# Feed-forwards 1 to 3 with the down projection between the gate and up units, in three fp32r passes, and modulation rows summed four to a tile

## The chip, the cores and the metric

The kernel runs on one NeuronCore of a Trainium2 chip (trn2). Its time is device microseconds of one launch, the median of several runs. A core has TensorE (matmuls into the 8 banks of PSUM), VectorE, ScalarE, GpSimd and SyncE; each works through its own list of instructions in order, and they wait for each other by semaphores. Loads are DMAs: a queue of SyncE, ScalarE or GpSimd issues one, and 16 DMA engines carry it.

## The reference, cut to what matters

Two transformer blocks in a row, each of two layers, over 256 tokens of width 1024, and 256 context tokens that only the first layer reads. All data is float32. Four SwiGLU feed-forwards belong to the first block:

```
def swiglu(h, w13, w2):                       # w13: 1024 x 5632, w2: 2816 x 1024
    a, b = jnp.split(h @ w13, 2, axis=-1)
    return (jax.nn.silu(a) * b) @ w2
def half_ffn(x, g, shift, scale, gate, w13, w2):
    return x + 0.5 * gate * swiglu(modulate(x, g, shift, scale), w13, w2)
m = (silu_c @ w_mod[i] + b_mod[i]).reshape(b, 1, N_MOD, d)     # shifts, scales and gates of a layer
```

Before the first layer's mixer a feed-forward runs over latent and context tokens (512 columns, "FFN 0"); FFN 1, 2 and 3 run over the 256 latent tokens. The modulation rows m are products of one vector with matrices of 1024 x 1024: 9 rows of each first-block layer, and 6 of each second-block layer. After them come mixers and, in the second block, two mixtures of experts (MoE) with 16 experts each.

## The kernel before

Activations lie with features on the partitions: X is 8 tiles of 128 features by up to 512 tokens. The order of the stages is fixed: first modulation rows, FFN 0, mixer a, FFN 1, FFN 2, mixer c, FFN 3, mixer e, MoE 0, mixer o, MoE 1. Between two stages stands a norm: VectorE updates X tile by tile, ScalarE squares, TensorE sums the squares (`mean_square`) and spreads the root, and VectorE and ScalarE write the normed h in two rounded parts (h high and h low).

Weights come through `ring`, four slots of 1 MB units (up to 1.4 MB). SyncE issues the load of a unit as soon as the unit four places ahead of it is done. A gate/up unit holds 128 gate and 128 up columns for all 8 feature tiles. It is split: ScalarE copies it, rounded to fp32r, into one of two buffers (L1437), and VectorE subtracts that from the unit in place (L1844), which gives the low part. TensorE then takes three fp32r products a tile, high x high, high x low and low x high (`up`, L777): 48 products of 128x128 with 256 columns a unit. There are 22 such units a feed-forward. ScalarE applies silu and VectorE multiplies gate and up parts into G.

After the 22 units come 8 down units of 1.4 MB, one for each output tile of 128 features. They are not split: one f32 product for each of 22 tiles of G (`down`, L850), which the page counts as two instructions each. FFN 0 already has its down part in three fp32r passes with split tiles (`down0`, L812); it stays as it is.

Besides, the modulation rows that are needed later are computed beside the feed-forwards. A row is a product of a vector of 1024 numbers with a 1024 x 1024 matrix, in 8 chunks of 128 matrix rows by 1024 columns (512 KB). SyncE loads a chunk into one of four buffers in CB (`chunk_in`, L577), after it has seen that the chunk four places before is added; VectorE adds chunk times a number for each partition to an accumulator of 128 x 1024 (`add_chunk`, L1878; for the three "dual" rows, which the context needs with a second vector, twice, L1868). When a row's 8 chunks are in, TensorE sums over the partitions by 8 f32 products with one column of ones (`column_sums`, L699, for dual rows 16, L709), and VectorE adds the bias (`take_row`). `CHUNKS_AT` says by hand how many chunks follow each unit; `PLAN` is made from it. There are 3 dual and 25 single rows, 224 chunks: 112 in FFN 0, 40 in FFN 1, 40 in FFN 2 and 32 in FFN 3. In SyncE's list the chunks of a unit stand behind the load of the unit two places later, in VectorE's behind the gate product of the unit and ahead of the split of a later one.

Of the kernel before, what the change touches and what calls it, by code (L numbers as in the profile page):

```python
# [7 lines left out]
ALU = mybir.AluOpType  # L8
# [6 lines left out]
P = 128  # L15
D = 1024
# [22 lines left out]
for _e in range(1, NE):  # L39
# [20 lines left out]
N_ROWS_C = 13  # L60
# [3 lines left out]
DOWN0 = _GROUPS + _GROUPS[4:] + _GROUPS[:4]  # L64
DOWN0_BANK = (0, 1, 5, 6, 2, 3, 4, 0)


N_DUAL_CHUNKS = N_DUAL * KT
# [7 lines left out]
ROW_ACC = (0, 1, 0, 1, 0, 1, 2, 0, 2, 0, 2, 0, 1, 0, 2, 3, 0, 1, 0, 2, 3, 0, 1, 2, 3)  # L76
ROW_BANK = tuple((4, 7)[r % 2] if r < 6 else 7 if r < 11 else (4, 6)[r % 2] for r in range(N_ROWS))


def chunk_plan():  # L80

    plan, n = [], 0
    for ups_at, downs_at in CHUNKS_AT:
        counts = list(ups_at) + list(downs_at)
        steps = [dict(chunks=[], sums=[], dual=[], takes=[]) for _ in counts]
        for i, count in enumerate(counts):
            for _ in range(count):
                steps[i]["chunks"].append(n)
                if n % KT == KT - 1:
                    r, at = n // KT - N_DUAL, min(i + 1, len(counts) - 2)  # L90
                    if r < 0:
                        steps[at]["dual"].append(r + N_DUAL)
                    else:
                        steps[at]["sums"].append(r)
                        steps[min(at + 1, len(counts) - 1)]["takes"].append(r)
                n += 1
        plan.append(steps)
    assert n == (N_DUAL + N_ROWS) * KT
# [6 lines left out]
def steps_after(n):  # L105

    return 2 * min(n + 1, N_DUAL_CHUNKS) + max(0, n + 1 - N_DUAL_CHUNKS)

# [3 lines left out]
    ("up1", FT), ("down1", KT), ("up2", FT), ("down2", KT), ("c_in", 8), ("c_out", 4),  # L112
    ("up3", FT), ("down3", KT), ("e_in", 14), ("e_out", 4), ("moe0", NE * 6),
# [21 lines left out]
for _name, _n in (("up0", FT), ("down0", len(DOWN0)), ("up1", FT), ("up2", FT), ("c_in", 8), ("up3", FT), ("e_in", 14), ("moe0", 6 * NE), ("o_in", 12),  # L135
# [15 lines left out]
for _name, _n in _COLS:  # L151
# [6 lines left out]
         ("rot_half", P), ("upper", P), ("ones", P), ("zeros", P), ("w4", 8), ("w16", 32), ("iota", CAP),  # L158
# [26 lines left out]
MOD_RUNS = ((0, N_FIRST * KT), (N_FIRST * KT, ROW_TILE0))  # L185
# [2210 lines left out]
```

## Time and profile before

| | |
|---|---|
| median of 3 runs (2500.26 to 2511.84) | 2507.69 us |
| the profiled execution's own time | 2501.64 us |
| its span, first to last instruction | 2499.8 us |
| busy: TensorE, VectorE, ScalarE | 96%, 57%, 40% |
| mean granted clock of TensorE, share of 2.4 GHz | 0.958 |
| moved by DMA, mean rate | 535.45 MB, 214 GB/s |
| PE L777 (gate/up), L850 (down), L699 (row sums), shares of the chain | 25%, 9%, 2% |
| FFN 0, from its first product to the mixer's first | 422 us |
| FFN 1, 2 and 3, up to the next stage's first product | 223, 223, 219 us |

The profile's shares of busy time are means over all stages. "PE" is TensorE's matmul, "PEld" its weight loads, "DVE" VectorE, "ACT" ScalarE, "SPq" the queue in which SyncE issues DMAs. The chain is the run of work that ended last, followed back step by step.

### The profile page before, as it was taken

What the parts mean: (1) busy time and instruction counts of PE and PEld (TensorE: products, weight loads), DVE (VectorE), ACT (ScalarE), POOL (GpSimd) and SP (SyncE); (2) the same over time, 40 slices, a digit from 0 to 9 for tenths busy, and PEclk for the clock granted to TensorE, in tenths of its full rate; (3) what the DMA queues carried; (4) which work ended last, traced back from release to release, by engine and by line L of the source; (5) the groups of instructions that cost most, each with busy time, mean ns of one, the idle gap of its engine ahead of it and who ended that gap; (6) DMA issues with size and microseconds to landing.
All of it is one profiled execution on the core that took longest, in us unless ns stands there. A gap on an engine that the chain in (4) does not pass through costs nothing.

```text
span 2499.8 us, 35746 instructions
## 1 busy us (share of the span) xinstructions
PE 2397.4 (96%) x15358; PEld 2158.7 (86%) x15358; DVE 1430.5 (57%) x1609; ACT 1000.5 (40%) x1257; POOL 4.5 (0%) x12
## 2 busy tenths in 40 slices
PE   9999999989999999999999988899999899899997
PEld 7788888867998999888998986899998888899996
DVE  0875676323763465234652442688887433888886
ACT  2211132214330332042321323577776344676774
POOL 0000000000000000000000000000000000000000
PEclk8999999989999999999999988899999789899998
DMA  7456767522777477543775431488886332488884
GB/s 277 172 196 240 265 227 271 192 68 79 259 279 277 171 292 294 186 152 129 262 276 212 151 118 37 148 300 294 300 305 242 142 121 75 179 304 295 296 307 180
DMA packets 94195, 535.45 MB, mean 214 GB/s; under 512 B 9984, under 2 KB 12296, under 8 KB 46800
## 3 DMA queue, kind: packets, MB, share of 16 engines
q1 hardware_dynamic: 92480, 524.33, 58.3%
q0 software_dynamic: 816, 5.65, 0.6%
q8 instruction: 126, 2.06, 0.3%
q10 hardware_dynamic: 736, 3.10, 0.3%
q14 instruction: 37, 0.30, 0.0%
HBM read 531.97 MB, written 1.06 MB: 213 GB/s over the span
## 4 chain that ended last, share of the span: by engine, by line
PE 90%; DVE 6%; ACT 3%; issue 1%; DVEq 0%; ACTq 0%
PE PS L777 25%; PE PS L1231 12%; PE PS L850 9%; PE PS L888 8%; PE PS L1259 7%; PE PS L812 5%; PE PS L935 5%; DVE moe_low L2202 2%; PE PS L1199 2%; PE PS L733 2%; PE PS L699 2%; PE PS L1179 1%; PE PS L659 1%; PE PS L742 1%; PE PS L876 1%
## 5 line engine op out<-in xcount | busy, mean ns | idle before, releaser
L777 PE MATMUL PS<-h_parts,ring_low 128*128 128x256 f32 (+1 forms) x1408 | 440.0, 313 | 0.0
L777 PE MATMUL PS<-h_parts,g_parts 128*128 128x256 f32 x2112 | 383.0, 284 | 0.9 <-DVE h_parts L1813 0.9
L2202 DVE TENSOR_TENSOR moe_low<-moe_ring,W_HIGH 128x2048 fp32r<-128x2048 f32 x128 | 292.9, 2290 | 83.1 <-ACT W_HIGH L1615 83.1
L777 PEld LDWEIGHTS PS<-h_parts,g_parts 128*128 128x128 f32 x2112 | 328.9, 192 | 2.4 <-issue 1.2
L1231 PE MATMUL PS<-moe_low,HXH 128*96 128x256 f32 x1024 | 287.9, 281 | 0.0
L777 PEld LDWEIGHTS PS<-h_parts,ring_low 128*128 128x128 f32 x1408 | 269.9, 192 | 16.1
L1615 ACT ACTIVATE W_HIGH<-moe_ring 128x2048 fp32r<-128x2048 f32 x128 | 244.5, 1912 | 23.4 <-PE PS L1259 22.7
L850 PE MATMUL PS<-G,ring 128*128 128x256 f32 x1056 | 236.5, 385 | 2.8 <-DVE G L1898 2.8
L850 PEld LDWEIGHTS PS<-G,ring 128*128 128x128 f32 x1056 | 201.3, 192 | 30.7 <-DVE G L1898 3.4
L1460 ACT ACTIVATE SG<-PS 128x256 f32<-128x256 f32 (+1 forms) x88 | 38.4, 437 | 462.9 <-PE PS L777 462.9
L1231 PEld LDWEIGHTS PS<-moe_low,HXH 128*96 128x96 f32 x1024 | 166.2, 162 | 0.3
L1898 DVE TENSOR_TENSOR G<-SG,PS 128x256 f32<-128x256 f32 (+1 forms) x88 | 43.0, 488 | 208.4 <-ACT SG L1460 208.4
L1844 DVE TENSOR_TENSOR ring_low<-ring,g_parts 128x2048 fp32r<-128x2048 f32 x66 | 150.9, 2291 | 18.8 <-ACT g_parts L1437 17.9
L2202 DVE TENSOR_TENSOR moe_low<-moe_ring,h_parts 128x2048 fp32r<-128x2048 f32 x64 | 146.3, 2286 | 4.0 <-ACT h_parts L1615 1.5
L1231 PE MATMUL PS<-W_HIGH,HXL 128*96 128x256 f32 x528 | 148.0, 280 | 0.0
L1231 PE MATMUL PS<-W_HIGH,HXH 128*96 128x256 f32 x528 | 148.0, 280 | 0.0
L1878 DVE SCALAR_TENSOR_TENSOR CAT<-CB,cond_rows,CAT 128x1024 f32<-128x1024 f32 x112 | 143.5, 1281 | 5.9
L777 PE MATMUL PS<-h_parts,W_HIGH 128*128 128x512 f32 x352 | 141.9, 403 | 3.5 <-DVE H_LOW L1809 3.5
L1231 PE MATMUL PS<-h_parts,HXH 128*96 128x256 f32 x496 | 142.4, 287 | 0.0
L777 PE MATMUL PS<-H_LOW,W_HIGH 128*128 128x512 f32 x352 | 141.5, 402 | 0.0
L1231 PE MATMUL PS<-h_parts,HXL 128*96 128x256 f32 x496 | 139.1, 280 | 0.0
L1437 ACT ACTIVATE g_parts<-ring 128x2048 fp32r<-128x2048 f32 x66 | 125.6, 1905 | 2.1 <-DMA ring<-up_w 2.1
(316 smaller groups left out, 4653.6 us busy)
## 6 DMA issues: line engine op xcount, KB each, us to landing
moe_ring<-moe_w SPq DMA_DIRECT2D x192, 1024.0 KB, 4.9
CB<-mod_rows SPq DMA_DIRECT2D x200, 512.0 KB, 5.9
ring<-up_w SPq DMA_DIRECT2D x88, 1024.0 KB, 5.0
ring<-lin_w SPq DMA_DIRECT2D x55, 1024.0 KB, 4.9
ring<-down_w SPq DMA_DIRECT2D x24, 1408.0 KB, 6.0
CB<-mod_dual SPq DMA_DIRECT2D x24, 512.0 KB, 4.1
ring<-down_w SPq DMA_DIRECT2D x10, 1024.0 KB, 7.8
ring<-mod_w SPq DMA_DIRECT2D x8, 1024.0 KB, 7.0
```

The lines of the kernel that those rows point to most:

```text
L777: return mm(dst(h), a[:, k, h * P:(h + 1) * P], b[:, k, :], start=start, stop=(k == KT - 1 and j == 2), skip_group_check=True)
L812: last = mm(PS[:, DOWN0_BANK[4 * half + d], :], a[:, t, d, :], b, start=(v % 6 + t + i == 0), stop=(final and t == len(tiles) - 1 and i == 2),
L850: last = mm(PS[:, i % 4, 0:S], ring[:, u % SLOTS, j * P:(j + 1) * P], G[:, j, 0:S], start=(j == 0), stop=(j == FT - 1))
L888: last = mm(dst, a, b, start=(k + j == 0), stop=(k + j == KT + len(pairs) - 2))
L935: last = mm(PS[:, i, c * S:(c + 1) * S], w[:, k, c * P:(c + 1) * P], CAT[:, k, :], start=(k == 0), stop=(k == KT - 1))
L1231: last = mm(PS[0:CAP, 2 + f % 2, 0:S], a[:, x], w[:, k, :], start=(k + i == 0), stop=(k + i == KT + 1))
L1259: last = mm(PS[0:CAP, n, :].rearrange("p (a c) -> p a c", a=2), x[:, part_g], w[:, cut, :], start=(h + f + i == 0), stop=(h + f + i == 4), ...
L1437: af(UP_HIGH[i % 2], by_tile(ring[:, u % SLOTS, 0:UW]), ACT.Copy).then_inc(w_high, 1)
L1615: af(w_high_tiles(p), by_tile(moe_ring[:, moe_slot(l, p), :]), ACT.Copy).then_inc(w_high, 1)
L1844: tt(by_tile(ring_low[:, u % SLOTS, 0:UW]), by_tile(ring[:, u % SLOTS, 0:UW]), UP_HIGH[i % 2], ALU.subtract).then_inc(w_low, 1)
L1878: stt(out=acc, in0=w, scalar=c, in1=acc, op0=ALU.mult, op1=ALU.add).then_inc(acc_steps, 1)
L2202: tt(by_tile(moe_low[:, moe_slot(l, p), :]), by_tile(moe_ring[:, moe_slot(l, p), :]), w_high_tiles(p), ALU.subtract).then_inc(w_low, 1)
```

## The change

Feed-forwards 1 to 3 (`FFN_UNITS`): four gate/up units, then nine times a down unit and two gate/up units, then the last two down units: 33 units of 1 MB. A down unit m holds the weights of two hidden tiles, 2m and 2m+1, for all 8 output tiles; its load takes eight pieces of 1 KB for a partition. Every unit is split into rounded parts, with four buffers for the high part instead of two (`FFN_HIGH`, in G's space). The product of gate and up is kept for six tiles only (`GATED`) and split as well, by a copy on ScalarE and a subtraction on VectorE. The down products take three fp32r passes and accumulate over all 11 down units in eight half banks of PSUM (`Y_BANK`). In the last unit the output tiles are finished one after another, and VectorE updates X meanwhile. Mean squares stand behind tile 6 of it (two) and behind it (six). The first two splits of the next stage move into the last two units.

Modulation rows: groups of four rows share an accumulator. A chunk now holds, for each of the four rows, 32 rows of its matrix, one row's part in 32 partitions each; a group takes 32 chunks, seven groups make 224 chunks. TensorE's sum for a group has four columns on the right (`block`), which add up 32 partitions each, so 8 products serve four rows (16 in group 0, where all four rows are computed with both vectors). The vector's numbers come in the new order by four small loads on GpSimd's queue (`cond_raw`). `CHUNKS_AT` is new: 104 chunks in FFN 0 and 40 in each other one. Nothing changes in the mixers and in MoE.

```diff
+ROWS, PARTS = 4, 32
+GROUP_CHUNKS = KT * P // PARTS
+N_GROUPS = (N_DUAL + N_ROWS) // ROWS
...
+FFN_UNITS = [("up", i) for i in range(4)]
+for _m in range(FT // 2 - 2):
+    FFN_UNITS += [("down", _m), ("up", 2 * _m + 4), ("up", 2 * _m + 5)]
+FFN_UNITS += [("down", FT // 2 - 2), ("down", FT // 2 - 1)]
+FFN_BUFFER0 = (0, 0, 33, 1)
+Y_BANK = ((4, 0), (4, 1), (5, 0), (5, 1), (6, 0), (6, 1), (7, 0), (2, 0))
...
-    ([3] * 8 + [4] * 9 + [3] * 4 + [0], [4] * 5 + [2] + [4, 2] + [4] * 3 + [0]),
-    ([1, 1, 2] * 6 + [1, 1, 0, 0], [3, 2, 3, 2, 2, 2, 0, 0]),
-    ([1, 1, 2] * 6 + [1, 1, 0, 0], [3, 2, 3, 2, 2, 2, 0, 0]),
-    ([1] * 20 + [0, 0], [2] * 6 + [0, 0]),
+    ([3] * 10 + [2] + [4] * 8 + [0, 4, 0], [4] * 5 + [2, 4, 2, 0, 4, 4, 0]),
+    ([1] * 4 + [2, 1, 1] * 5 + [0, 1, 1] + [2, 1, 1] * 3 + [2, 0], []),
+    ([1] * 4 + [2, 1, 1] * 3 + [0, 1, 1] + [2, 1, 1] * 5 + [2, 0], []),
+    ([2] * 4 + [0, 1, 1] + [2, 1, 1] * 7 + [2] + [0] * 4, []),
...
             def chunk_in(n):
-                src = mod_dual[n] if n < N_DUAL_CHUNKS else mod_rows[n - N_DUAL_CHUNKS]
+
+                g, k, part = n // GROUP_CHUNKS, n % GROUP_CHUNKS // ROWS, slice(n % ROWS * PARTS, (n % ROWS + 1) * PARTS)
                 if n >= 4:
                     sp.wait_ge(acc_steps, steps_after(n - 4))
-                sp.dma_start(ROWS_W[:, n % 4, :], src).then_inc(rows_full[n % 4], 16)
+
+                def put(j, rows, src):
+                    dst = ROWS_W[j * PARTS:(j + rows) * PARTS, n % 4, :]
+                    sp.dma_start(dst, src).then_inc(rows_full[n % 4], 16)
+                if g == 0:
+                    put(0, N_DUAL, mod_dual[k::KT, part, :])
+                    put(N_DUAL, 1, mod_rows[k:k + 1, part, :])
+                else:
+                    r0 = ROWS * (g - 1) + 1
+                    put(0, ROWS, mod_rows[r0 * KT + k:(r0 + ROWS - 1) * KT + k + 1:KT, part, :])
 
             def ffn(f):
...
+                    kind, at = FFN_UNITS[i]
+                    if kind == "up":
+                        return UW, source(up_w, FT * f + at)
+                    part = down_w[KT * f:KT * (f + 1), :, 2 * at * P:2 * (at + 1) * P]
+                    return UW, part.rearrange("d p n -> p d n")
...
+            def column_sums(g):
+                pe.wait_ge(acc_steps, steps_after((g + 1) * GROUP_CHUNKS - 1))
+                wait(pe, rows_taken, g)
+                for j in range(1 if g else 2):
+                    acc = ACC if g else DUAL_ACC[:, j, :]
+                    for d in range(KT):
+                        at = j * ROWS * KT + d
+                        last = mm(PS[:, GROUP_BANK[g], at:at + 3 * KT + 1:KT], acc[:, d * P:(d + 1) * P],
+                                  tab("block")[:, 0:ROWS], start=True, stop=True)
                 last.then_inc(colsum_done, 1)
 
-            def dual_column_sums(r):
...
+                        high, low = down_tiles(high), down_tiles(low)
+                        def products(t, d):
+                            j = 2 * i + t
+                            pe.wait_ge(g_low, FT * f + j + 1)
+                            (bank, half), at = Y_BANK[d], j % 6
+                            pairs = ((high, GATED_HIGH), (high, GATED_LOW), (low, GATED_HIGH))
+                            for p, (a, b) in enumerate(pairs):
+                                last = mm(PS[:, bank, half * S:(half + 1) * S], a[:, t, d, :], b[:, at, :],
+                                          start=(j + p + half == 0), stop=(j == FT - 1 and p == 2),
+                                          skip_group_check=True)
+                            return last
+                        if i < FT // 2 - 1:
+                            for t in range(2):
+                                for d in range(KT):
+                                    last = products(t, d)
+                        else:
+                            for d in range(KT):
+                                for t in range(2):
+                                    last = products(t, d)
+                                if d in (1, 3, 5, 6):
+                                    last.then_inc(y0_psum, 1)
+                                if d == 6:
+                                    mean_square(AFTER_DOWN[f], 0)
+                                    mean_square(AFTER_DOWN[f], 1)
                     last.then_inc(unit_done, 1)
-                    if i:
-                        mean_square(AFTER_DOWN[f], i - 1)
...
+                    sums(f, n)
+                for d in range(2, KT - 1):
+                    mean_square(AFTER_DOWN[f], d)
...
+            def ffn(f):
+
+                def gated_high(i):
+                    act.wait_ge(g_ready, FT * f + i + 1)
+                    af(GATED_HIGH[:, i % 6, :], GATED[:, i % 6, :], ACT.Copy).then_inc(g_high, 1)
+                units = len(FFN_UNITS)
+                for n, (kind, i) in enumerate(FFN_UNITS):
+                    if n + 2 < units:
+                        split(f, n + 2)
+                    else:
+                        split_next(f, n + 2 - units)
+                    if n and FFN_UNITS[n - 1][0] == "up":
+                        gated_high(FFN_UNITS[n - 1][1])
+                    if kind == "up":
+                        act.wait_ge(unit_done, UNIT0[f"ffn{f}"] + n + 1)
+                        af(SG[:, i % 4, 0:S], PS[:, i % 2, 0:S], ACT.Silu).then_inc(silu_ready, 1)
 
...
+            for part in range(ROWS):
+                src = bass.AP(cols_in.tensor, part * PARTS * NCOLS, [[0, ROWS], [NCOLS, PARTS], [1, 4 * KT]])
+                pool.dma_start(cond_raw[:, part, :], src).then_inc(ld_cond, 16)
...
+                for j in range(1 if g else 2):
+                    acc = ACC if g else DUAL_ACC[:, j, :]
+                    at = 4 * (m // ROWS) + (group_cond(g) if g else j)
+                    c = cond_rows[:, m % ROWS, at:at + 1]
+                    if m == 0:
+                        if g > 1:
+                            dve.wait_ge(colsum_done, g)
+                        ts(acc, w, c, None, ALU.mult).then_inc(acc_steps, 1)
+                    else:
+                        dve.wait_ge(acc_steps, steps_after(n - 1) if g else 2 * n - 1 + j)
+                        stt(out=acc, in0=w, scalar=c, in1=acc, op0=ALU.mult, op1=ALU.add).then_inc(acc_steps, 1)
...
+                def gated_low(i):
+                    dve.wait_ge(g_high, FT * f + i + 1)
+                    tt(GATED_LOW[:, i % 6, :], GATED[:, i % 6, :], GATED_HIGH[:, i % 6, :], ALU.subtract).then_inc(g_low, 1)
+                units = len(FFN_UNITS)
+                for n, (kind, i) in enumerate(FFN_UNITS):
+                    if n + 2 < units:
+                        split(f, n + 2)
+                    else:
+                        split_next(f, n + 2 - units)
+                    if n and FFN_UNITS[n - 1][0] == "up":
+                        gated_low(FFN_UNITS[n - 1][1])
+                    if kind == "up":
+                        dve.wait_ge(silu_ready, FT * f + i + 1)
+                        tt(GATED[:, i % 6, :], SG[:, i % 4, 0:S], PS[:, i % 2, S:2 * S], ALU.mult).then_inc(g_ready, 1)
+                    if n == units - 2:
+                        gate_columns(f)
+                    rows_step(PLAN[f][n])
+                for d in range(KT):
+                    if d == KT - 1:
+                        dve.wait_ge(unit_done, UNIT0[f"ffn{f}"] + units)
+                    else:
+                        dve.wait_ge(y0_psum, 6 + 4 * (f - 1) + (1, 1, 2, 2, 3, 3, 4)[d])
+                    bank, half = Y_BANK[d]
+                    update(f, d, bank, half * S)
 
             def gate_columns(f):
                 N = NORMS[FFNS[f][0]][0]
```

## Rows read from the trace of the kernel before

**Rows 1.** The page, busy us of each engine.

```profile
PE 2397.4 (96%) x15358; PEld 2158.7 (86%) x15358; DVE 1430.5 (57%) x1609; ACT 1000.5 (40%) x1257; POOL 4.5 (0%) x12
```

**Rows 2.** Windows: stretch, length, busy by engine, PEclk, DMA share, GB/s.

```profile
65.60:339.70 274.10, 274.08 (x1249) 225.31 (x1250) 184.20 (x173) 57.35 (x57) 0.00 (x0) 0.97 0.63 219
...
626.90:760.60 133.70, 132.78 (x1104) 132.06 (x1103) 88.91 (x84) 47.82 (x49) 0.00 (x0) 1.00 0.75 273
...
836.00:838.00 2.00, 2.00 (x6) 1.56 (x5) 0.37 (x2) 0.00 (x0) 0.00 (x0) 0.50 0.45 174
```

**Rows 3.** The chain in order of time: start us, us, what.

```profile
112.69 3.47 PE PS L709 x32
...
154.27 24.63 PE PS L777 x96
...
375.02 22.45 PE PS L812 x96
...
399.15 22.40 PE PS L812 x96
...
487.63 7.14 PE PS L876 x32
...
626.89 40.63 PE PS L777 x336
...
705.75 34.87 PE PS L777 x288
...
742.30 17.39 PE PS L777 x144
...
760.60 19.26 PE PS L850 x88
...
780.20 9.60 PE PS L850 x44
...
833.49 11.29 PE PS L850 x44
...
849.48 41.11 PE PS L777 x336
...
1072.56 6.33 PE PS L876 x48
...
1170.80 52.41 PE PS L777 x432
...
1389.76 6.33 PE PS L876 x48
```

**Rows 4.** VectorE from 626 to 1400 us: group | busy us, mean ns.

```profile
L1844 DVE TENSOR_TENSOR ring_low<-ring,g_parts 128x2048 fp32r<-128x2048 f32 x64 | 146.4, 2291 | 16.5 <-ACT g_parts L1437 15.6
...
L1878 DVE SCALAR_TENSOR_TENSOR CAT<-CB,cond_rows,CAT 128x1024 f32<-128x1024 f32 x56 | 71.6, 1279 | 1.3
...
L1898 DVE TENSOR_TENSOR G<-SG,PS 128x256 f32<-128x256 f32 x66 | 27.8, 421 | 122.6 <-ACT SG L1460 122.6
```

**Rows 5.** DMA issues: count, KB each, median us to landing.

```profile
CB<-mod_rows SPq DMA_DIRECT2D x200, 512.0 KB, 5.9
...
ring<-down_w SPq DMA_DIRECT2D x2, 512.0 KB, 6.7
```

**Rows 6.** Timeline of the issuing queues: start us, us, queue, line.

```profile
1.19 0.47 ACTq L1699 DMA_DIRECT2D X<-x_in  x1
...
2.17 1.03 ACTq L1702 DMA_DIRECT2D H<-rel_in  x1
...
52.26 2.06 SPq L577 DMA_DIRECT2D CB<-mod_dual  x3
```

**Rows 7.** Two windows as in rows 2, and DMA packets, 367 to 368 us.

```profile
4.00:24.00 20.00, 20.00 (x70) 13.29 (x69) 0.24 (x2) 8.53 (x14) 0.00 (x0) 1.00 1.02 423
...
350.00:360.00 10.00, 10.00 (x45) 8.04 (x44) 9.75 (x11) 4.00 (x5) 0.00 (x0) 1.00 0.93 312
...
DMA packets 275, 0.35 MB, mean 345 GB/s; under 512 B 13, under 2 KB 250, under 8 KB 275
```

More of the change, by code:

```diff
@@ L84, in chunk_plan @@
         counts = list(ups_at) + list(downs_at)
-        steps = [dict(chunks=[], sums=[], dual=[], takes=[]) for _ in counts]
+        steps = [dict(chunks=[], sums=[], takes=[]) for _ in counts]
         for i, count in enumerate(counts):
@@ L88, in chunk_plan @@
                 steps[i]["chunks"].append(n)
[L89 to L95, printed above, removed]
+                if n % GROUP_CHUNKS == GROUP_CHUNKS - 1:
+                    steps[i + 1]["sums"].append(n // GROUP_CHUNKS)
+                    steps[i + 2]["takes"].append(n // GROUP_CHUNKS)
                 n += 1
         plan.append(steps)
-    assert n == (N_DUAL + N_ROWS) * KT
+    assert n == N_GROUPS * GROUP_CHUNKS
     return plan
@@ L1870, in add_chunk @@
-                r, k = q // KT, q % KT
-                c, acc = cond_flat[:, q:q + 1], ACC[ROW_ACC[r]]
-                if k == 0:
-                    wait(dve, colsum_done, max([0] + [o + 1 for o in range(r) if ROW_ACC[o] == ROW_ACC[r]]))
-                    ts(acc, w, c, None, ALU.mult).then_inc(acc_steps, 1)
-                else:
-                    dve.wait_ge(acc_steps, steps_after(n - 1))
-                    stt(out=acc, in0=w, scalar=c, in1=acc, op0=ALU.mult, op1=ALU.add).then_inc(acc_steps, 1)
@@ new lines, in take_group @@
+            def take_group(g):
+                dve.wait_ge(colsum_done, g + 1)
+                at = ROW_TILE0 + (g * ROWS - N_DUAL) * KT
+                bias = COL["mod_b"].start + at
+                if g == 0:
+                    line(tt(M[:, at:at + N_DUAL * KT, 1], PS[:, GROUP_BANK[0], ROWS * KT:(ROWS + N_DUAL) * KT],
+                            cols[:, bias:bias + N_DUAL * KT], ALU.add))
+                tt(M[:, at:at + ROWS * KT, 0], PS[:, GROUP_BANK[g], 0:ROWS * KT], cols[:, bias:bias + ROWS * KT], ALU.add)\
+                    .then_inc(rows_taken, 1)
+                dve.wait_ge(rows_taken, g + 1)
+                line.wait()
@@ L1888, in up, with rows_step, up0 @@
+            def rows_step(step):
+                for g in step["takes"]:
+                    take_group(g)
+                for n in step["chunks"]:
+                    add_chunk(n)
+            def up0():
                 for i in range(FT):
-                    step = PLAN[f][i]
-                    if i and (f == 0 or i + 1 < FT):
-                        split(f, i + 1)
-                    if f == 0 and i == FT - 1:
+                    if i:
+                        split(0, i + 1)
+                    if i == FT - 1:
@@ L2309, in _ @@
             norm(5)
-            up(3)
-            down(3)
+            ffn(3)
             norm(6)
```

358 lines of the change are left out of this document (150 added, 208 removed).

## The prediction

> **What bounds the kernel now.** I read the busy line and the stage windows first, then the chain of waits, then the DMA issues. TensorE is busy for 96% of the span [rows 1], and in the windows of FFN 0 and FFN 1 it is busy without a gap while VectorE works 184.20 of 274.10 and 88.91 of 133.70 us [rows 2]. The chain is almost one run of TensorE pieces: 48 fp32r products of a gate/up unit go at 34.87/288 = 0.121 us each, so a unit takes 5.81 us; 44 instructions of an f32 down unit take 9.6 us [rows 3]. Between pieces stand column sums: 3.47 us for a two-row sum of a dual row, and 742.30 - (705.75 + 34.87) = 1.68 us for a single row [rows 3]. The DMA is at 0.75 of its time in FFN 1 and 0.63 in up 0 [rows 2]. So the kernel is bound by TensorE now, with a third of VectorE and a quarter or more of the DMA in hand.
>
> **What TensorE gains.** I sum against the profiled execution (2501.6 us; the median of the runs shown is 2507.7, 6 above it).
>
> Down projections: 19.26 + 6 x 9.60 = 76.9 us a feed-forward becomes 11 units x 5.81 = 63.9, since an fp32r triple of products has the form of the gate/up ones. Three times 13.0 = -39.0.
>
> Column sums: 25 x 1.68 + 3 x 3.47 = 52.4 us become six groups of 1.68 and a double one of 3.47 = 13.6, as 16 instructions serve four rows. A right operand of 4 columns instead of 1 I cost at nothing, because weights are loaded alike. -38.8.
>
> Clock: behind the last sums of the dual rows 96 instructions took 24.63 instead of about 22.4, and one down unit with a sum and mean squares ahead took 11.29 instead of 9.60, once more in FFN 2 [rows 3]; the granted clock stood at 0.50, the lower of its two levels (1.2 GHz), at 836 to 838 us [rows 2], after such products. I take -5 for what goes away of it, and +3 for new dips: the norm after a feed-forward has five mean squares in a row where two stood.
>
> The step from the gate/up part to the first down unit (760.60 - 742.30 - 17.39 = 0.91 us [rows 3]) goes three times: -2.7. The mean squares leave the gaps between down units and come back in the tail: 0. Each pair of products now waits for its g_low: in down 0 two units with such waits take 22.45 and two without 22.40 [rows 3], so 0 here, at worst 0.1 us each, 528 x 0.1 = 53.
>
> Handoffs: a down unit with two ups asks VectorE for 3 x 2.29 (splits) + 4 x 1.28 (rows) + 4 x about 0.42 = 13.7 of 17.4 us [rows 4]; hidden, with four buffers to even it out. A unit of FFN 0 with three dual chunks asks 6 x 1.28 + 2.3 for the split + 0.7 for the gate product of 512 columns = 10.7 [rows 4], against 22.4/2 = 11.2 on TensorE [rows 3]: hidden, with half a microsecond to spare. The four small loads of cond_raw on GpSimd's queue lie under the wait for X. Loading h and gates otherwise stays.
>
> TensorE alone would so give 2501.6 - 82 = 2420 us.
>
> **What the DMA is asked for.** This is the step on which my forecast rests. A chunk of modulation rows is 512 KB both before and after. Before, source and destination run over 128 rows or partitions on the outside. After, the source is four blocks of 32 rows, 4 MB apart, so the outermost level counts 4, and in group 0 it is one transfer with 3 blocks and one with 32 rows. If a transfer is dealt to the 16 DMA engines along its outermost level, a chunk can use 4 engines (3 for the large part of group 0) instead of 16. In the trace all heavy transfers have 128 outside, so it cannot show this directly. The nearest row is the load of the bias table, the only one on a hardware queue with fewer than 16 on the outside (8 partitions): its issue takes 1.03 us for 6 KB, where that of X takes 0.47 for 2 MB [rows 6]. It is dealt out differently; I take it as a sign.
>
> [...]
>
> Price. With 4 engines each carries 524,288/4 = 131 KB a chunk; in group 0 131 KB and 8 KB of the second transfer, 139 KB. A weight unit still brings 65.5 KB to each engine. The speed of one engine: 423/16 = 26.4 GB/s over 20 us at the start, full; 312/0.93/16 = 21 in down 0 with 4 KB and 2 KB pieces [rows 7]. I take 25.5, nearer the first, since four engines ask less of the memory; 28 and 22 are my ends, the first a little above what any stretch shows.
>
> FFN 0: 32 x 139 + 72 x 131 + 31 x 65.5 KB = 15.9 MB on the busiest engine = 625 us. The first chunks are issued at 52.26 [rows 6] behind a weight unit; from 55 us on, and with about 12 us left after the last chunk, the next stage starts at 692 instead of 487.6 [rows 3], +204.
>
> FFN 1 and 2: two chunks and three units are in before the start; 38 x 131 + 30 x 65.5 KB = 6.95 MB = 272 us, then 12 for the last split, eight updates and the norm: 284.5 against 849.48 - 626.89 = 222.6 and 223.1 [rows 3]: +62 each.
>
> FFN 3: the last chunk stands in step 28 of 33: 36 x 131 + 28 x 65.5 KB = 6.55 MB = 257 us, then four units at 5.81 and the norm, 287 against 219.0 [rows 3]: +68.
>
> Nothing of TensorE's gain is left in these stages, because its 191 us a feed-forward lie under 272 of DMA. The chunk adds stand in VectorE's order before the next unit's split, SyncE waits for the add of chunk n - 4 before it issues chunk n, and with it all later weight loads; so late chunks hold TensorE. TensorE's half clock in the gaps (5.81 us would become up to 11.6) is inside the DMA's time. Sum: 2501.6 + 204 + 124 + 68 = **2897 us**. At 28 GB/s it is 2770, at 22 about 3115.
>
> The down units come in 1 KB pieces. Down 0 has such a unit (2 x 512 KB, 6.7 us to landing [rows 5]), and the microsecond in which its pieces went moved 345 GB/s [rows 7]. So no cost.
>
> **Rivals.**
> A. The chunks still use all 16 engines. Then the sum of TensorE holds: 2420 us, to 2460 if waits or late splits cost up to 1 us in each of 33 down units. For it: no row shows a narrow transfer that is slow; the mean demand, 5.24 MB a triple of 17.4 us or 301 GB/s, is below the 423 of rows 7. Against: the slow issue. This is the side of "faster"; it decides when a chunk reaches more than 7 engines or so, as then a chunk brings 75 KB to an engine, and 104 x 75 + 31 x 65.5 KB = 9.8 MB are within the 10.6 MB that one moves in FFN 0's 416 us.
>
> B. 16 engines, but blocks 4 MB apart and pieces of 1 KB lower the rate to 240 GB/s in FFN 1 to 3: 55.6 MB each need 232 us instead of 192, so 2420 + 3 x 40 = 2540. Against it are rows 7.
>
> C. The change doesn't do what it says for the down products: an fp32r product with G as right operand costs what f32 does. Then A gives 2459. The gate/up rows speak against it.
>
> **Chances.** The forecast 0.85, A with C 0.11, B 0.04. Within the forecast 0.95 lie in 2760 to 3130, which is the range and holds 0.81 in all. Half a percent, 12.5 us, is what a measurement can tell here: faster 0.11, same 0.01, slower 0.88.
>
> **What would show it.** DMA share in FFN 0 near 0.35 with 140 to 160 GB/s, and a median of over 15 us from issue to landing for mod_rows (5.9 now [rows 5]); TensorE busy about half of FFN 0 and two thirds of FFN 1 to 3; VectorE's idle time ended by the DMA of CB; issue of a chunk near 1 us. MoE and mixers unchanged. Right in any case: 11 x 5.81 us of products a down part, and seven column sums. If mod_rows lands in 6 us and FFN 1 takes about 200 us, the dealing is wrong and A holds.

## The result and the profile after

The changed kernel takes 3154.45 us (median, 3145.04 to 3165.64); the kernel before takes 2507.15 us in the runs beside it. The ratio is 1.259, 95% interval [1.254, 1.264]. I had forecast 2897 us with a range up to 3130: the direction and the place are right, the size is not, and the time is just outside the range.

The page of the kernel after first: TensorE's line (it was busy 96% [rows 1]), the chain by engine and by line, and two of the costliest groups with the idle time before them and what ended it.

```profile
PE 2481.7 (79%) x15518; PEld 2245.2 (71%) x15518; DVE 1549.9 (49%) x1697; ACT 1085.2 (35%) x1355; POOL 7.3 (0%) x16
...
PE 43%; DMA 40%; DVE 7%; SPq 6%; ACT 2%; issue 1%; DVEq 0%; ACTq 0%
DMA CB<-mod_rows 36%; PE PS L1291 10%; PE PS L948 6%; PE PS L1319 6%; SPq L607 5%; DMA ring<-up_w 4%; PE PS L995 4%; PE PS L873 2%; DVE moe_low L2274 2%; DVE roots L1939 2%; PE PS L1259 2%; PE PS L763 1%; PE PS L1239 1%; PE PS L699 1%; PE PS L772 1%
...
L1939 DVE SCALAR_TENSOR_TENSOR roots<-CB,cond_rows,roots 128x1024 f32<-128x1024 f32 x186 | 238.9, 1284 | 470.9 <-DMA CB<-mod_rows 468.0
L1487 ACT ACTIVATE FFN_HIGH<-ring 128x2048 fp32r<-128x2048 f32 x99 | 189.0, 1911 | 699.8 <-DMA ring<-up_w 372.0
```

The chain was TensorE's; now 40% of it is DMA, nearly all of that the chunks of modulation rows. VectorE waits 468 us for them, in the very instruction that adds a chunk. The DMA issues answer to [rows 5]. The page gives the chunks no landing time here. The first line is the gate/up units' before, the other two are after (count, KB, median us to landing).

```profile
ring<-up_w SPq DMA_DIRECT2D x88, 1024.0 KB, 5.0
...
ring<-up_w SPq DMA_DIRECT2D x88, 1024.0 KB, 18.6
...
ring<-down_w SPq DMA_DIRECT2D x43, 1024.0 KB, 24.3
```

Windows of the kernel after, with the columns of [rows 2]: 325 us of FFN 0, the three other feed-forwards whole, and 2 us each of two moments in FFN 2.

```profile
66.40:391.00 324.60, 221.63 (x835) 176.67 (x836) 152.33 (x140) 45.15 (x44) 0.00 (x0) 0.81 0.40 128
891.20:1239.20 348.00, 235.40 (x1660) 230.14 (x1660) 151.39 (x147) 86.22 (x97) 0.00 (x0) 0.81 0.54 161
1239.20:1594.40 355.20, 237.56 (x1661) 232.72 (x1660) 151.02 (x146) 85.89 (x97) 0.00 (x0) 0.81 0.53 155
1689.90:2037.90 348.00, 244.14 (x1708) 238.87 (x1709) 153.73 (x153) 89.14 (x102) 1.44 (x2) 0.82 0.55 165
1439.00:1441.00 2.00, 1.55 (x7) 1.55 (x8) 0.73 (x2) 0.00 (x0) 0.00 (x0) 0.50 0.24 98
1450.00:1452.00 2.00, 2.00 (x14) 2.00 (x13) 1.29 (x2) 0.00 (x0) 0.00 (x0) 0.64 0.90 233
```

FFN 1, 2 and 3 take 348.0, 355.2 and 348.0 us where they took 222.6, 223.1 and 219.0 [rows 3]: +125, +132, +129. The last two rows are what matters most. At 1439 us a quarter of the DMA is busy and moves 98 GB/s, which is 25 GB/s for each of four engines. At 1450 us 90% of it is busy and moves only 233 GB/s, which is 16 GB/s for each of 16. Before the change a full DMA gave 423 [rows 7].

The same in the DMA line over 34 us of FFN 2, 1432 to 1466, about one round of four chunks and three weight units (4.74 MB moved; a round is 5.24). The first line is the share in tenths, the second the GB/s, 40 slices each.

```profile
DMA  9999993222222222222225999992222223222486
GB/s 239 229 229 241 236 217 96 96 116 92 116 92 67 96 92 111 111 106 101 82 116 153 299 224 229 224 176 69 92 92 111 96 106 114 101 93 87 87 139 212
```

Twos are chunks alone on four engines, nines weight units beside a chunk. The chain of waits at this place and at the starts of two stages (start us, us, what):

```profile
751.89 7.14 PE PS L936 x32
...
1398.55 32.13 DMA CB<-mod_rows
1430.68 0.02 issue
1430.70 1.29 DVE roots L1939
1431.99 0.41 SPq L607
...
1432.44 32.89 DMA CB<-mod_rows
```

It is a closed circle: SyncE issues a chunk, the chunk lands 33 us later behind three others and three weight units, VectorE adds it (1.29 us), which frees the buffer, and SyncE issues the next. One turn, with a triple of units on which TensorE works 17.4 us, takes 1432.44 - 1398.55 = 33.9 us. The mixer starts at 751.89 instead of 487.63 [rows 3], so FFN 0 costs 264 us more. Sum: 264 + 125 + 132 + 129 = 650; the two profiled spans differ by 3143.2 - 2499.8 = 643. The other stages differ little: mixer a took 139.3 us and takes 139.3, mixer c 98.2 and 95.5, and from mixer e to the end it is 1110.0 and 1105.3.

### The profile page after: what moved, and what is told of

Read it like the earlier page. It is cut to its first block, busy times and chain, and to the rows that moved or that the text cites. A ratio compares the mean times of both kernels' runs of the same rounds, so it can differ in the third digit from the quotient of the medians.

```text
span 3143.2 us, 36264 instructions
## 1 busy us (share of the span) xinstructions
PE 2481.7 (79%) x15518; PEld 2245.2 (71%) x15518; DVE 1549.9 (49%) x1697; ACT 1085.2 (35%) x1355; POOL 7.3 (0%) x16
## 4 chain that ended last, share of the span: by engine, by line
PE 43%; DMA 40%; DVE 7%; SPq 6%; ACT 2%; issue 1%; DVEq 0%; ACTq 0%
DMA CB<-mod_rows 36%; PE PS L1291 10%; PE PS L948 6%; PE PS L1319 6%; SPq L607 5%; DMA ring<-up_w 4%; PE PS L995 4%; PE PS L873 2%; DVE moe_low L2274 2%; DVE roots L1939 2%; PE PS L1259 2%; PE PS L763 1%; PE PS L1239 1%; PE PS L699 1%; PE PS L772 1%
## 5 line engine op out<-in xcount | busy, mean ns | idle before, releaser
L873 PE MATMUL PS<-h_parts,FFN_HIGH 128*128 128x256 f32 x2112 | 420.8, 301 | 67.5 <-DVE ring_low L1908 66.9
L1939 DVE SCALAR_TENSOR_TENSOR roots<-CB,cond_rows,roots 128x1024 f32<-128x1024 f32 x186 | 238.9, 1284 | 470.9 <-DMA CB<-mod_rows 468.0
L1487 ACT ACTIVATE FFN_HIGH<-ring 128x2048 fp32r<-128x2048 f32 x99 | 189.0, 1911 | 699.8 <-DMA ring<-up_w 372.0
L873 PEld LDWEIGHTS PS<-h_parts,FFN_HIGH 128*128 128x128 f32 x2112 | 357.4, 208 | 75.8 <-DVE ring_low L1908 75.1
L1908 DVE TENSOR_TENSOR ring_low<-ring,FFN_HIGH 128x2048 fp32r<-128x2048 f32 x99 | 226.8, 2292 | 349.8 <-ACT FFN_HIGH L1487 349.8
L895 PE MATMUL PS<-GATED_HIGH,FFN_HIGH 128*128 128x256 f32 x528 | 178.1, 337 | 231.1 <-DVE ring_low L1908 183.0
L873 PE MATMUL PS<-h_parts,ring_low 128*128 128x256 f32 x1056 | 314.3, 298 | 0.0
L895 PE MATMUL PS<-GATED_LOW,FFN_HIGH 128*128 128x256 f32 x528 | 171.9, 326 | 0.0
L895 PE MATMUL PS<-GATED_HIGH,ring_low 128*128 128x256 f32 x528 | 170.7, 323 | 0.0
L798 PE MATMUL PS<-h_parts,ring_low 128*128 128x512 f32 x352 | 151.2, 430 | 0.0
```

The lines of the kernel that those rows point to most:

```text
L798: return mm(PS[:, 2 * (i % 2) + h, :], a[:, k, h * P:(h + 1) * P], b[:, k, :], start=(k + j == 0), stop=(k == KT - 1 and j == 2), skip_gro ...
L873: return mm(PS[:, i % 2, h * S:(h + 1) * S], a[:, k, h * P:(h + 1) * P], b[:, k, :], start=start, stop=(k == KT - 1 and j == 2), skip_grou ...
L895: last = mm(PS[:, bank, half * S:(half + 1) * S], a[:, t, d, :], b[:, at, :], start=(j + p + half == 0), stop=(j == FT - 1 and p == 2), sk ...
L1487: af(ffn_high(f, n)[:, 0:width], ring[:, u % SLOTS, 0:width], ACT.Copy).then_inc(w_high, 1)
L1908: tt(ring_low[:, u % SLOTS, 0:width], ring[:, u % SLOTS, 0:width], ffn_high(f, n)[:, 0:width], ALU.subtract)\
L1939: stt(out=acc, in0=w, scalar=c, in1=acc, op0=ALU.mult, op1=ALU.add).then_inc(acc_steps, 1)
```

## The experiments

Each kernel is told as an edit to the changed one, if nothing else is said. Times are medians in us; ratios are to the kernel before, with the 95% interval where there were several rounds.

| kernel | a chunk is brought in by | us | ratio |
|---|---|---|---|
| changed | 4 blocks of 32 rows, 4 MB apart | 3154.5 | 1.259 [1.254, 1.264] |
| e1_whole | 128 rows in a row | 2410.6 | 0.962 [0.958, 0.965] |
| e2_padded | 4 blocks of 32 rows, 132 KB apart | 3152.6 | one run |
| e3_interleaved | 32 rows outside, 4 blocks 4 MB apart inside | 2404.4 | 0.960 [0.957, 0.964] |
| e4_fourloads | 4 transfers, each to 32 neighbouring partitions | 2513.3 | one run |
| e5_strided | 4 transfers, each to every fourth partition | 2416.3 | 0.966 [0.963, 0.968] |
| e6_eight | 8 blocks of 16 rows | 2693.5 | 1.074 [1.071, 1.076] |
| e7_whole_down | as e1_whole, down units contiguous too | 2412.7 | 0.964 [0.963, 0.966] |
| e8_before_narrow | kernel before, 4 blocks of 32 rows, 4 MB apart | 3139.7 | one run |
| e9_halves | 2 transfers, each to 64 neighbouring partitions | 2507.9 | 1.004 [1.002, 1.007] |
| e10_sixteen | 16 blocks of 8 rows | 2501.5 | 1.001 [0.999, 1.002] |
| e11_thirtytwo | 32 blocks of 4 rows | 2413.7 | 0.965 [0.961, 0.968] |
| e12_alternate | 2 transfers, even and odd partitions | 2413.4 | 0.964 [0.960, 0.967] |

### Is it the shape of the source? (e1_whole)

```diff
-                else:
-                    r0 = ROWS * (g - 1) + 1
-                    put(0, ROWS, mod_rows[r0 * KT + k:(r0 + ROWS - 1) * KT + k + 1:KT, part, :])
+                sp.dma_start(ROWS_W[:, n % 4, :], mod_rows[n]).then_inc(rows_full[n % 4], 16)
```

> The changed kernel, with one edit: the host lays the 224 chunks of modulation rows out one after the other, each as 128 rows of 4 KB, so that a chunk is one transfer with 128 on the outside, as before the change; the same numbers go to the same partitions. If the four blocks on the outermost level are what costs the time (theory: four of 16 engines carry a chunk), the time falls to TensorE's own sum, 2420 to 2460 us, mod_rows lands in about 6 us, FFN 1 takes about 205 us instead of 348. If the down units' 1 KB pieces or the new order of waits are the cause (rival), it stays above 2800 us. If the grouping is right but the 1 KB pieces lower the rate, about 2540 us.

Measured 2410.6 us. So the whole loss hangs on how a chunk's source is laid out and read, and without it TensorE's gain shows. This kernel also beats the kernel before by 3.8%. Its page (TensorE's line and two issues) and windows: 100 us in FFN 1, then the four feed-forwards whole.

```profile
PE 2311.5 (96%) x15518; PEld 2108.8 (87%) x15518; DVE 1544.7 (64%) x1697; ACT 1083.6 (45%) x1355; POOL 7.3 (0%) x16
...
CB<-mod_rows SPq DMA_DIRECT2D x224, 512.0 KB, 5.8
ring<-up_w SPq DMA_DIRECT2D x88, 1024.0 KB, 4.9
```

```profile
640.00:740.00 100.00, 100.00 (x837) 100.00 (x836) 72.29 (x62) 40.75 (x42) 0.00 (x0) 1.00 0.80 289
...
66.53:451.75 385.22, 384.69 (x1743) 318.92 (x1743) 282.06 (x268) 94.66 (x101) 2.14 (x4) 0.98 0.65 232
591.08:795.79 204.71, 203.80 (x1660) 203.37 (x1660) 150.31 (x147) 86.25 (x97) 0.00 (x0) 0.97 0.76 273
795.79:998.82 203.03, 200.46 (x1658) 199.88 (x1658) 149.44 (x145) 85.64 (x96) 0.00 (x0) 0.99 0.75 270
1097.27:1301.20 203.93, 203.93 (x1676) 203.88 (x1677) 150.36 (x148) 86.13 (x97) 1.44 (x2) 0.98 0.76 271
```

TensorE has no gap in the 100 us, and the DMA moves 289 GB/s in 0.80 of its time.

### Number of engines or distance in DRAM? (e2_padded, e3_interleaved)

e2_padded is e1_whole with a source of four blocks that stand close together, and with the same outermost 4 in group 0 too (the host's new layout is not shown, here and below):

```diff
-                sp.dma_start(ROWS_W[:, n % 4, :], mod_rows[n]).then_inc(rows_full[n % 4], 16)
+                sp.dma_start(ROWS_W[:, n % 4, :], mod_rows[n, :, 0:PARTS, :]).then_inc(rows_full[n % 4], 16)
```

> The changed kernel, but the four blocks of 32 rows of a chunk stand 132 KB apart in DRAM (one unused row of 4 KB behind each block) instead of 4 MB; the outermost level still counts 4, in all groups alike. Theory 1, that a chunk goes to four engines because of its outermost level, and that the slow mixed phases come from those engines writing and reading beside the others: it stays slow, 3050 to 3200 us, with the DMA at 220 to 240 GB/s where weight loads run beside a chunk and about 100 GB/s where a chunk is alone. Theory 2, that the blocks' distance of 4 MB slows the memory in the mixed phases: the mixed phases reach about 400 GB/s and the time falls to what I had forecast, 2850 to 2950 us. If the narrow outermost level is not the cause at all, about 2440 us.

Measured 3152.6 us: theory 1. Its window of FFN 1 shows the same 0.54 and some 160 GB/s as the changed kernel:

```profile
900.00:1230.00 330.00, 207.78 (x1484) 202.72 (x1483) 134.62 (x119) 73.15 (x78) 0.00 (x0) 0.82 0.54 159
```

e3_interleaved turns it round: the blocks stay 4 MB apart, but the rows of a block go outermost. The column sums' table and the four small loads of the vector follow the new order of partitions.

```diff
+                src = mod_rows[g * ROWS * KT + k:(g * ROWS + ROWS - 1) * KT + k + 1:KT, part, :].rearrange("r p n -> p r n")
+                sp.dma_start(ROWS_W[:, n % 4, :], src).then_inc(rows_full[n % 4], 16)
```

> The changed kernel, but the four rows of a chunk lie interleaved over the partitions (partition 4p + j holds row j), so that the outermost level of the transfer counts 32; the blocks in DRAM stand 4 MB apart as in the changed kernel, every packet is still 4 KB. If a chunk is dealt out along its outermost level, it reaches all 16 engines and the time is that of the contiguous chunks, 2420 to 2460 us. If the distance of 4 MB between neighbouring packets lowers the rate, it lies 40 to 400 us above the kernel with contiguous chunks.

Measured 2404.4 us, no different from e1_whole, and so is its window of FFN 1:

```profile
640.00:740.00 100.00, 100.00 (x837) 100.00 (x836) 71.40 (x62) 38.90 (x41) 0.00 (x0) 1.00 0.80 288
```

So the 4 MB cost nothing with 32 outermost (2404.4 us against 2410.6), and taking them away gains nothing with 4 (3152.6 against 3154.5). Between these kernels the outermost level decides.

The packet records show the number of engines without naming them. While only 4 KB packets are under way in FFN 1, there are exactly four at once for 84% of that time in the changed kernel and 86% in e2_padded, eight for 71% in e6_eight (below), and 16 or 17 for 53% in e1_whole and 57% in e3_interleaved.

### Are narrow chunks the whole cause? (e8_before_narrow)

```diff
-                src = mod_dual[n] if n < N_DUAL_CHUNKS else mod_rows[n - N_DUAL_CHUNKS]
+                src = mod_rows[n % 176:n % 176 + 25:8, 32 * (n % 4):32 * (n % 4 + 1), :]
```

> The kernel before, with one edit: the source of each of the 224 chunks is four blocks of 32 rows, 4 MB apart, in the same array of modulation matrices. It reads other rows of these matrices than the computation needs, so the modulation values are not the reference's; the number of chunks, bytes, adds and column sums is the same. If narrow chunks are all that made the changed kernel slow, the four feed-forwards lose here what they lost there or somewhat more, since TensorE's gains are missing but lie under the DMA: 3100 to 3250 us. If the new order of units, the 1 KB pieces or the four buffers had a share, it stays below 3000 us.

Measured 3139.7 us. The kernel before, in all else as it was, becomes as slow as the changed one. Its window over the same stretch of FFN 0 has the same share and rate:

```profile
66.40:391.00 324.60, 232.31 (x912) 187.41 (x912) 139.72 (x136) 43.76 (x45) 0.00 (x0) 0.82 0.40 129
```

So neither the new order of units nor the four buffers is needed for the slowness. This is one run.

### Do the 1 KB pieces of the down units cost anything? (e7_whole_down)

```diff
-                    part = down_w[KT * f:KT * (f + 1), :, 2 * at * P:2 * (at + 1) * P]
-                    return UW, part.rearrange("d p n -> p d n")
+                    return UW, source(down_units, FT // 2 * (f - 1) + at)
```

> The kernel with contiguous chunks, and besides the host lays out the down units of FFN 1 to 3 contiguously, 128 rows of 8 KB, instead of picking them out of the matrix in 1 KB pieces. If 1 KB pieces cost nothing, as I predicted, the time is that of the contiguous chunks within 0.3% (ratio to the kernel before 0.962, +-0.004) and only the landing falls from 5.5 to 4.9 us. If they hold the path, it is 10 to 40 us faster.

Measured 2412.7 us, ratio 0.964 [0.963, 0.966], against 0.962 [0.958, 0.965]. The pieces cost nothing, as predicted. The same 100 us of FFN 1 carry the same bytes in 0.78 of the DMA's time instead of 0.80:

```profile
640.00:740.00 100.00, 100.00 (x837) 100.00 (x836) 72.34 (x62) 39.94 (x42) 0.00 (x0) 1.00 0.78 289
```

### Why 3154 and not 2897: from how many engines on is it hidden? (e6_eight)

The one thing that my sum didn't give was the 233 GB/s of a busy DMA. Eight blocks instead of four test it: by the dealing alone they are hidden.

```diff
-                sp.dma_start(ROWS_W[:, n % 4, :], mod_rows[n]).then_inc(rows_full[n % 4], 16)
+                sp.dma_start(ROWS_W[:, n % 4, :], mod_rows[n, :, 0:P // 8, :]).then_inc(rows_full[n % 4], 16)
```

> The changed kernel, but a chunk is one transfer of eight blocks of 16 rows (each followed by one unused row in DRAM), so that the outermost level counts 8. In the prediction I had put the point from which narrow transfers are hidden at 7 engines. By the dealing alone each of eight engines carries 65.5 KB a chunk, 38 x 65.5 + 30 x 65.5 KB = 4.45 MB in FFN 1, 175 us at 25.5 GB/s and hidden under TensorE's 192: 2410 to 2440 us. If the packets of such a transfer also slow the weight loads beside them, as in the changed kernel (14 to 15 GB/s an engine), the same bytes take about 300 us and the time is 2600 to 2800 us.

Measured 2693.5 us: the second. By its bytes and 25.5 GB/s an engine has 175 us of work in FFN 1, and the kernel still loses some 280 us to e1_whole. 100 us of FFN 1:

```profile
700.00:800.00 100.00, 88.11 (x682) 87.05 (x680) 56.13 (x49) 30.11 (x31) 0.00 (x0) 0.93 0.83 233
```

The share is as high as in e1_whole, the rate 233 instead of 289. The DMA takes longer for the same bytes. In the trace's packet records of 200 us of FFN 1 (640 to 840 us in e1_whole, 700 to 900 in e6_eight), a 4 KB packet takes 159 ns at the median in e1_whole and 214 in e6_eight, an 8 KB packet 309 and 396.

### What makes a packet slow? (e4_fourloads, e5_strided)

Four transfers of 32 rows each use all 16 engines by the dealing; e3_interleaved, with 32 outermost, had 16 or 17 packets at once. In e4_fourloads row j goes to 32 neighbouring partitions, in e5_strided to every fourth (with the sums' table and the small loads of e3_interleaved):

```diff
 # e4_fourloads
+                for j in range(ROWS):
+                    dst = ROWS_W[j * PARTS:(j + 1) * PARTS, n % 4, :]
+                    sp.dma_start(dst, mod_rows[(g * ROWS + j) * KT + k, part, :]).then_inc(rows_full[n % 4], 16)
 # e5_strided: the same, but
+                    dst = ROWS_W[j:P:ROWS, n % 4, :]
```

> The changed kernel, but a chunk is brought in by four transfers of 32 partitions each, one for each row, instead of one transfer with four blocks; DRAM as in the changed kernel. Each transfer has 32 on the outside. Theory of the dealing: all 16 engines carry it, two packets of 4 KB each; the time is that of the contiguous chunks plus what three more issues a chunk cost on SyncE (0.5 us each, hidden unless SyncE is late): 2420 to 2500 us. If a transfer that reaches only 32 partitions is slow as such, it stays above 2800 us.

> As the kernel with four transfers of 32 partitions a chunk, but with the partitions of the interleaved kernel: row j of a chunk goes to partitions j, j + 4, j + 8 ..., so that each transfer of 32 rows reaches all of SBUF instead of 32 neighbouring partitions. Count, size, source and issue of the transfers are those of the four-transfer kernel (2513 us, 4 KB packets at a median of 273 ns instead of 159 where weights load beside them). [...] Theory 2, that four small transfers cost more than one large one, by their issues and their pieces: it stays at 2490 to 2530 us.

Measured 2513.3 us for e4_fourloads, beyond the range of its theory, and 2416.3 for e5_strided, far below the 2490 of theory 2. So it is not the number of transfers or their size that costs the 97 us between them. The 100 us of FFN 1, first e4_fourloads:

```profile
640.00:740.00 100.00, 90.75 (x718) 89.09 (x718) 63.89 (x56) 34.19 (x34) 0.00 (x0) 0.97 0.99 253
```

and e5_strided:

```profile
640.00:740.00 100.00, 100.00 (x836) 100.00 (x836) 72.81 (x62) 39.22 (x39) 0.00 (x0) 1.00 0.82 288
```

Count, size and source of the chunk transfers are equal. Only the partitions written differ, and with them the DMA goes from full at 253 GB/s to 0.82 at 288. The packet records say it once more: 4 KB at a median of 271 ns in the first, 159 in the second. So it is the place of writing in SBUF that makes packets slow here. Why, no record shows.

### Two transfers, near and far (e9_halves, e12_alternate)

```diff
 # e9_halves
+                for j in range(2):
+                    dst = ROWS_W[P // 2 * j:P // 2 * (j + 1), n % 4, :]
+                    sp.dma_start(dst, mod_rows[n, P // 2 * j:P // 2 * (j + 1), :]).then_inc(rows_full[n % 4], 16)
 # e12_alternate: the same, but
+                    sp.dma_start(ROWS_W[j:P:2, n % 4, :], mod_rows[n, j:P:2, :]).then_inc(rows_full[n % 4], 16)
```

> The kernel with contiguous chunks, but each chunk in two transfers, to partitions 0 to 63 and 64 to 127, 256 KB each, both wide enough for 16 engines. [...] If only the count of transfers or partitions matters, half of the loss at most: 2410 to 2460 us.

> As the kernel with two transfers of 64 partitions a chunk (2508 us), but one transfer takes the even partitions and one the odd ones, so that each reaches all of SBUF. Theory 1: it is enough that a transfer reaches all of SBUF: 2400 to 2430 us, as with the four strided transfers (2416 us). [...]

Measured 2507.9 us for the halves, above the 2410 to 2460 that the count of transfers or partitions alone would give: 64 neighbouring partitions are as bad as 32 (2513.3 us). Measured 2413.4 for even and odd: theory 1. The rows, e9_halves:

```profile
640.00:740.00 100.00, 93.63 (x750) 92.82 (x749) 65.77 (x57) 36.15 (x37) 0.00 (x0) 0.97 1.01 259
```

and e12_alternate:

```profile
640.00:740.00 100.00, 100.00 (x837) 100.00 (x836) 71.21 (x62) 39.46 (x41) 0.00 (x0) 1.00 0.83 290
```

### Sixteen and 32 blocks (e10_sixteen, e11_thirtytwo)

One transfer again, to all 128 partitions, from blocks with one unused row behind each.

```diff
 # e10_sixteen
+                sp.dma_start(ROWS_W[:, n % 4, :], mod_rows[n, :, 0:P // 16, :]).then_inc(rows_full[n % 4], 16)
 # e11_thirtytwo
+                sp.dma_start(ROWS_W[:, n % 4, :], mod_rows[n, :, 0:4, :]).then_inc(rows_full[n % 4], 16)
```

> As the kernel with eight blocks a chunk (2694 us), but with sixteen blocks of 8 rows, each followed by one unused row in DRAM; the outermost level counts 16. If the number on the outermost level sets the engines, all 16 carry a chunk, and the time is that of the contiguous chunks, 2400 to 2430 us. If a source in blocks is what is slow, it is above 2500 us.

> As the kernel with sixteen blocks of 8 rows a chunk (2501.5 us), but with 32 blocks of 4 rows, each followed by one unused row in DRAM; the outermost level counts 32, as in the interleaved kernel, and each block goes to four neighbouring partitions. [...] Theory 2: a source in blocks with gaps is slow, and the interleaved kernel is fast for another reason: 2490 to 2520 us.

e10_sixteen took 2501.5 us, and by the count of engines I had expected 2400 to 2430. It reaches all partitions, with all engines (16 or 17 packets at once for 55% of the time in which only 4 KB packets are under way), and is still slow. The other theory on record, that a source in blocks is what is slow, put it above 2500. Its 100 us of FFN 1:

```profile
640.00:740.00 100.00, 89.97 (x722) 88.14 (x721) 63.97 (x55) 34.40 (x35) 0.00 (x0) 0.98 1.00 251
```

With 32 blocks, gaps and all, it is fast, 2413.7 us, outside the 2490 to 2520 of theory 2, so a source in blocks isn't slow as such:

```profile
640.00:740.00 100.00, 100.00 (x837) 100.00 (x836) 71.39 (x62) 38.43 (x40) 0.00 (x0) 1.00 0.81 288
```

So a full count of engines on all partitions is not enough: e10_sixteen and e11_thirtytwo both have 16 or 17 packets at once for most of the time with 4 KB packets alone, both write all 128 partitions, and their 4 KB packets take 276 and 159 ns at the median. They differ in their blocks, 8 rows to 8 neighbouring partitions against 4 rows to 4. What I infer is that it counts which of the partitions each engine writes. No record names the engine of a packet, so this is my inference and not shown.

## Why the prediction was right or wrong

**What TensorE gains: right.** I summed 2420 us for the kernel without a DMA limit; e1_whole takes 2410.6 and e3_interleaved 2404.4. Stage by stage e1_whole has 385.2, 204.7, 203.0 and 203.9 us against 422.0, 222.6, 223.1 and 219.0 before [rows 2, 3]: -36.8, -17.9, -20.1 and -15.1, together -89.9, and 8 more than my -82. By my own terms FFN 0 was to give about 24 and FFN 1 to 3 about 58 together; they gave 37 and 53. So the good sum is in part luck: two errors stand against each other in it. The chain of e1_whole in FFN 0, in FFN 1 and at the end of it:

```profile
66.53 134.38 PE PS L790 x576
200.91 3.47 PE PS L733 x32
204.38 88.81 PE PS L790 x384
293.18 1.68 PE PS L733 x16
294.87 21.94 PE PS L790 x96
...
614.18 5.76 PE PS L887 x48
619.94 11.52 PE PS L865 x96
...
706.34 1.69 PE PS L733 x16
...
784.49 0.83 PE PS L887 x6
785.32 4.03 PE PS L755 x20
...
795.79 23.03 PE PS L865 x192
```

- Down products: 5.76 us a unit where I had 5.81, so 11 x 5.76 = 63.4 instead of 76.9 us. Rival C is out.
- Column sums: six of 1.68 and one of 3.47 us, as summed. Four columns instead of one cost nothing that shows at 16 instructions.
- FFN 0 gained 36.8 us, of which the sums are 23.1: three double ones (3.47, 4.49 and 3.47) and eleven of 1.68 went, 3.47 and two of 1.68 came. My sum took all double ones at 3.47.
- Clock: the 96 products behind two of the double sums took 24.63 [rows 3] and 23.86 us, at a granted clock of 0.91 and 0.93; the other pieces of 96 took 22.40 to 22.50. That is 3.6 of the other 13.7 us. In e1_whole the first twelve units take 134.38/6 = 22.40 us for 96 products, the next eight 22.20, and the last two, which stand behind a sum as they did before, 21.94. The clock of the last is 1.00, and it was 1.00 in the pieces of 22.4 before, so the clock doesn't explain this part. Why they run 2% faster I don't know.
- Mean squares "come back in the tail: 0" was too good. From the last down product to the next stage it is 795.79 - 785.32 = 10.5 us in FFN 1, and was 849.48 - (833.49 + 11.29) = 4.7 [rows 3]. This is most of why FFN 1 to 3 gained less than summed.
- Waits and late splits: 0, as taken, or nearly. TensorE is busy 203.80 of 204.71 us in FFN 1 of e1_whole, and 200.46 of 203.03 in FFN 2.

**The dealing: right.** That a chunk uses four engines, and three in group 0, was an assumption of my sum that no row of the kernel before shows. The packets under way at once in the changed kernel agree with it: while only 4 KB packets are under way, exactly four at once for 84% of that time in FFN 1, and exactly three for 84% from 66 to 250 us, where the chunks of group 0 run. In the changed kernel the DMA is at 0.24 and 98 GB/s while only chunks run; e2_padded keeps that with the blocks close together, and e1_whole, e3_interleaved and e11_thirtytwo lose it with 128 or 32 outermost. The sign I went by, the slow issue of a small narrow load [rows 6], proved little. The three-block transfers of the changed kernel are issued in 0.73 to 0.77 us at their quickest and its four-block ones in 0.55, against a median of 0.43 for a chunk in FFN 1 of e1_whole; but e10_sixteen, with all 16 engines, needs 0.54 for a chunk as well. That the sign pointed the right way was luck.

**The speed of one engine: this step failed.** "I take 25.5, nearer the first, since four engines ask less of the memory; 28 and 22 are my ends". By the prediction's own formula (bytes of the busiest engine, over the stage without its ends) the measured stages give 15.9 MB in 685 us = 23.2 GB/s in FFN 0, and 6.95 MB in 336 us = 20.7, 6.95 in 343 = 20.3 and 6.55 in 318 = 20.6 in FFN 1, 2 and 3: three of four under my low end. The 25.5 holds while the four are alone (98 GB/s / 4 = 25). It doesn't hold while weight units run beside a chunk: then all 16 together move mostly 217 to 241 GB/s, some 14 an engine, and the weight units slow down with the chunk. In the packet records of FFN 1 an 8 KB packet takes 309 ns at the median when 16 or more packets are under way and no chunk packet is among them, and 554 with four of them. The chunk's own 4 KB packets take 159 ns while at most five packets are under way, and 267 with 16 or more; in e1_whole they take 159 in both cases. A turn of four chunks and three units is 721 KB on a busy engine: at 25.5 GB/s 28.3 us, measured 33.9. Over the nine and a half rounds of FFN 1 that is 53 of the 63 us by which the delay, 125, exceeds my 62.

I had weighed the engines' speed by what the memory gives, and not by what they write to. e4_fourloads against e5_strided and e9_halves against e12_alternate show that the place of writing alone can take the DMA from 288 and 290 GB/s at shares of 0.82 and 0.83 to 253 and 259 at 0.99 and 1.01. That the changed kernel's mixed phases have the same cause, and not another that comes with few engines, rests on one more step: e6_eight, e10_sixteen and e4_fourloads have 8, 16 and 16 engines, and all show long packets (4 KB at a median of 214, 276 and 271 ns, where the changed kernel's mixed phases have 267). No run has four engines and short packets beside weight units, so this last step is inferred and not shown. The range was short of it too: my sum at 22 GB/s gives 3125 us and not the 3115 that I wrote, still under the 3154.

**The point of rival A: wrong for the same reason.** "It decides when a chunk reaches more than 7 engines or so." With 8 engines the kernel takes 2693.5 us, with sixteen blocks and 16 engines 2501.5; only the forms whose 4 KB packets take 159 ns reach 2404 to 2416. So it was not decided by the bytes for each engine.

**Rival B is out:** blocks 4 MB apart cost nothing in e3_interleaved, 1 KB pieces nothing in e7_whole_down.

**The stages.** FFN 0 was to cost +204 and cost +264; FFN 1, 2 and 3 +62, +62 and +68, and cost +125, +132 and +129. The error of the sum is 650 - 396 = 254 us. I put it down to this one term, since the changed kernel's other stages took what they took before or a few us less, and its delays go away with the narrow transfers (e1_whole).

**The signs.** The DMA share in FFN 0 is 0.40 (I said 0.35) at 128 GB/s (140 to 160). TensorE is busy in 0.68 of FFN 0 (I said half) and 0.67 to 0.70 of the others (two thirds). VectorE's idle time is ended by the DMA of CB, 468 us of it. The issue of a chunk was to take about 1 us: the quickest take 0.55, but the median is 2.4 and the longest 19.57. This is its queue in the changed kernel (start us, us, queue, line):

```profile
1431.06 2.68 SPq L607 DMA_DIRECT2D CB<-mod_rows  x2
1433.78 15.57 SPq L589 DMA_DIRECT2D ring<-down_w  x1
1449.40 12.66 SPq L607 DMA_DIRECT2D CB<-mod_rows  x1
```

One down unit keeps SyncE for 15.57 us; in e1_whole it takes 0.38. So behind slow chunks the issuing is slow as well, and the weight units also start late. What SyncE waits for inside an issue no record shows.

## What to carry to other kernels

Look at the outermost level of every heavy transfer after a change of layout: here 4 on it went with four packets at once, 8 with eight, and 16, 32 or 128 with 16 or 17 (84%, 71%, and 53 to 61% of the time with 4 KB packets alone), and a transfer that looks tidier in the source made this kernel a quarter slower (3154.5 us against 2507.2). The count is not enough, though. Transfers with 32, 64 or 128 outermost that spread over all of SBUF were fast here (2404.4 to 2416.3 us, 4 KB packets at 159 ns); 32 or 64 neighbouring partitions at a time, or 4, 8 or 16 blocks, took 2501.5 to 3154.5 us and also slowed what ran beside them (8 KB packets of weight units at medians of 396 to 471 ns in FFN 1, against 309). Here the reordered layout on the host kept all of the change's gain (0.962 of the time before), and so did another order of the same access pattern, with the rows left where they were (0.960).

## What the runs showed that I had not expected

- Blocks of rows on the outermost level: 4 give 3153 us, 8 give 2694, 16 give 2502, 32 give 2414, 128 rows 2411. All have the same bytes and 4 KB packets.
- A narrow transfer slows others: an 8 KB packet of a weight unit takes 309 ns with no chunk packet beside it and 400, 505, 529 and 554 with one to four (medians in FFN 1 of the changed kernel, with 16 or more packets under way).
- Sixteen engines at once can be a full DMA at 251 GB/s (e10_sixteen) or at 0.80 with 289 (e1_whole), for the same bytes to the same partitions.
- SyncE spends up to 15.57 us on issuing a unit beside narrow transfers, which takes 0.38 in e1_whole.
- The time of an issue doesn't tell the number of engines: 0.55 us for four blocks, 0.54 for sixteen.
